# Opening of a fused decoder step: slots and banks of the first two tiles, place of the narrow tile, size of the first pieces, and who moves the raw tiles out

## The reference

```
n = x * rsqrt(mean(x * x) + 1e-6) * g_mix          # D = 2048
proj = n @ w_in     # 5,216 columns: q, k, v, qi, ki, wi (indexer), qb, kb, vb, gb, rb (GLA), uc, vc (gMLP)
```

## Time and profile before

| | |
|---|---|
| median of three runs | 1409.0 us (1406.78 to 1410.85) |
| the profiled execution, time | 1407.28 us |
| the profiled execution, span from first to last instruction | 1405.6 us |
| TensorE busy | 1393.0 us |
| VectorE busy | 850.4 us |
| ScalarE busy | 578.7 us |
| granted TensorE clock, mean | 1.00 |

### The profile page before, as it was taken

How to read it: one execution, slowest core, us unless ns; L and a number is a source line. 1 busy time by engine, 2 the same in 40 slices (tenths; PEclk the granted TensorE clock), 3 DMA queues, 4 the chain that set the end, 5 groups by cost and what they waited for, 6 DMA issues and landing times.

```text
span 1405.6 us, 28379 instructions
## 1 busy us (share of the span) xinstructions
PE 1393.0 (99%) x10632; PEld 1375.3 (98%) x10632; DVE 850.4 (61%) x1175; ACT 578.7 (41%) x696; POOL 118.8 (8%) x178
## 2 busy tenths in 40 slices
PE   7999999999999999999999999999999999999998
PEld 7999989999999999999999999999999999999998
DVE  6668767646876555555554444555555556666554
ACT  6545743565334333333333333333333333335332
POOL 1314105000221000000000000000000001111000
PEclk9999999999999999999999999999999999999999
DMA  8847434446544544544445556444544445556553
GB/s 281 226 154 241 164 123 136 147 130 233 178 155 156 179 165 157 173 158 168 156 147 164 165 163 199 158 168 157 171 157 168 159 131 164 164 164 201 176 161 117
DMA packets 76134, 236.69 MB, mean 168 GB/s; under 512 B 13800, under 2 KB 14456, under 8 KB 75704
## 3 DMA queue, kind: packets, MB, share of 16 engines
q1 hardware_dynamic: 71424, 223.59, 48.3%
q0 software_dynamic: 3776, 11.54, 2.7%
q10 hardware_dynamic: 888, 0.93, 0.2%
HBM read 231.48 MB, written 4.47 MB: 168 GB/s over the span
## 4 chain that ended last, share of the span: by engine, by line
PE 98%; DMA 1%; DVE 1%; SPq 0%; ACT 0%; issue 0%; DVEq 0%
PE acc L495 31%; PE acc L497 31%; PE acc L496 31%; PE px L1611 1%; DMA proj<-in_xT 1%; PE px L1496 0%; PE px L1574 0%; PE px L1555 0%; DMA w_raw<-in_w_in 0%; PE px L495 0%; PE px L497 0%; PE px L496 0%; DVE x_lo L1003 0%; PE px L1680 0%; PE px L1567 0%; PE px L1531 0%
## 5 line engine op out<-in xcount | busy, mean ns | idle before, releaser
L445 DVE TENSOR_TENSOR w_lo<-w_raw,w_hi 128x1024 fp32r<-128x1024 f32 (+3 forms) x446 | 507.7, 1143 | 315.6 <-ACT w_hi L439 307.0
L439 ACT ACTIVATE w_hi<-w_raw 128x1024 fp32r<-128x1024 f32 (+3 forms) x446 | 439.5, 989 | 562.7 <-PE acc L497 551.3
L495 PE MATMUL acc<-n_hi,w_hi 128*128 128x288 f32 x1664 | 492.8, 296 | 0.0
L496 PE MATMUL acc<-n_lo,w_hi 128*128 128x288 f32 x1664 | 490.9, 295 | 0.0
L497 PE MATMUL acc<-n_hi,w_lo 128*128 128x288 f32 x1664 | 489.3, 294 | 0.0
L497 PEld LDWEIGHTS acc<-n_hi,w_lo 128*128 128x128 f32 x1664 | 313.5, 188 | 0.0
L496 PEld LDWEIGHTS acc<-n_lo,w_hi 128*128 128x128 f32 x1664 | 312.4, 188 | 0.1
L495 PEld LDWEIGHTS acc<-n_hi,w_hi 128*128 128x128 f32 x1664 | 311.8, 187 | 0.1
L495 PE MATMUL acc<-x_hi,w_hi 128*128 128x288 f32 x816 | 246.5, 302 | 1.0 <-DVE w_lo L445 1.0
L496 PE MATMUL acc<-x_lo,w_hi 128*128 128x288 f32 x816 | 240.8, 295 | 0.0
L497 PE MATMUL acc<-x_hi,w_lo 128*128 128x288 f32 x816 | 240.1, 294 | 0.0
(11 more groups left out here) (283 smaller groups left out, 861.0 us busy)
## 6 DMA issues: line engine op xcount, KB each, us to landing
w_raw<-in_w_gu SPq DMA_DIRECT2D x176, 512.0 KB, 3.8
w_raw<-in_w_in SPq DMA_DIRECT2D x76, 512.0 KB, 4.3
w_raw<-in_w_down SPq DMA_DIRECT2D x64, 384.0 KB, 3.0
w_raw<-in_w_down SPq DMA_DIRECT2D x64, 320.0 KB, 3.0
w_raw<-in_w_ple SPq DMA_DIRECT2D x32, 576.0 KB, 3.8
w_raw<-in_w_out SPq DMA_DIRECT2D x32, 512.0 KB, 4.2
w_raw<-in_w_in SPq DMA_DIRECT2D x12, 256.0 KB, 6.7
proj<-in_xT SPq DMA_DIRECT2D x4, 576.0 KB, 7.5
```

Of the source, the lines that this page charges most:

```text
L439: nc.scalar.activation(whi[:, slot, 0:kt * P], raw[:, slot, 0:kt * P], ACT.Copy).then_inc(S("w_hi_done"), 1)
L445: nc.vector.tensor_tensor(wlo[:, slot, 0:kt * P], raw[:, slot, 0:kt * P], whi[:, slot, 0:kt * P].bitcast(F32), ALU.subtract).then_inc(S("w ...
L495: nc.tensor.matmul(out, w_h, row_of(m_hi_, k0 + k), start=first and k == 0, stop=False)
L496: nc.tensor.matmul(out, w_h, row_of(m_lo_, k0 + k), start=False, stop=False)
```

## The change

- The gains are loaded by ScalarE's queue under a semaphore of their own, so `small_loaded` counts to 16.
- `BEGIN` cuts the first x piece in two: rows 0 and 1 with a quarter of tile 0, rows 2 and 3 with one of tile 1. TensorE waits for each row by itself, and begins with blocks 0 and 1 of tile 0.
- The quarters of the first two tiles use the slots in the order of use: slot 0 has the first two quarters of tile 0, slot 1 those of tile 1, slots 2 and 3 the second two. The counts of `w_lo_done` and `w_used` follow.
- Tiles 0 and 1 accumulate in banks of `px`; tile 2 in `acc` bank 1, tile 3 in bank 0.
- The narrow tile is the fourth (tile 3) instead of the third; `ki` lands in turn 3.
- ScalarE moves tiles 0, 1 and 2 out unscaled, between squares and roundings, and calls Ln once on a dummy before the root.
- VectorE scales the three raw rows in one instruction, which counts `acc_read` up by 3. The remainder of chunk 8 now precedes the last squares.
- `mean_squares(0)` moves from behind chunk 6 to the middle of chunk 8.
- `weights` and SyncE's copy wait for `acc_read` of the `ki` tile, which is 4.

```diff
@@ -46,10 +46,10 @@
-ORDER = (ROW_QI, ROW_QI + 1, ROW_KI, *range(ROW_QI + 2, ROW_QI + 8), *range(ROW_K, ROW_K + 4), *range(ROW_Q, ROW_Q + 8),
+ORDER = (ROW_QI, ROW_QI + 1, ROW_QI + 2, ROW_KI, *range(ROW_QI + 3, ROW_QI + 8), *range(ROW_K, ROW_K + 4), *range(ROW_Q, ROW_Q + 8),
...
-SOURCE = (0, 1, MISC_TILE, *range(2, 8), *range(18, 22), *range(10, 18), *range(22, N_ROWS))
+SOURCE = (0, 1, 2, MISC_TILE, *range(3, 8), *range(18, 22), *range(10, 18), *range(22, N_ROWS))
...
@@ -312,7 +312,7 @@
-        SQ = ROW_QI + 2
+        SQ = ROW_QI + 3
...
@@ -445,21 +445,19 @@
+        BEGIN = [(0, 2, [(0, 0)]), (2, 4, [(1, 0)])] + [(4 * c, 4 * c + 4, [(0, c), (1, c)]) for c in range(1, 4)]
         def quarter(weights, t, c):
...
-            return weights[:, 2 * t + c // 2, (c % 2) * 4 * P:(c % 2 + 1) * 4 * P]
+            return weights[:, 2 * (c // 2) + t, (c % 2) * 4 * P:(c % 2 + 1) * 4 * P]
...
         def quarter_hi(t, c):
...
-        QUARTER_LO = {(0, 0): ("quarter_lo", 1), (1, 0): ("quarter_lo", 2), (0, 1): ("w_lo_done", 1), (1, 1): ("quarter_lo", 3),
-                      (0, 2): ("quarter_lo", 4), (1, 2): ("quarter_lo", 5), (0, 3): ("w_lo_done", 2), (1, 3): ("w_lo_done", 4)}
         def quarter_lo(t, c):
...
-            name, value = QUARTER_LO[t, c]
-            return S(name), value
+            return (S("w_lo_done"), c + t) if c % 2 else (S("quarter_lo"), c + t + 1)
...
@@ -543,13 +541,11 @@
-            sp.dma_start(gains[:, :, :], a["gains"]).then_inc(S("small_loaded"), 16)
-            for c in range(4):
-                sp.dma_start(x_f[:, 4 * c:4 * c + 4, :], a["xT"][:, 4 * c:4 * c + 4, :]).then_inc(S(f"x_loaded{c}"), 16)
-                for t in range(2):
+            for k0, k1, parts in BEGIN:
+                sp.dma_start(x_f[:, k0:k1, :], a["xT"][:, k0:k1, :]).then_inc(S(f"x_loaded{k0}"), 16)
+                for t, c in parts:
...
-                        .then_inc(loaded[2 * t + c // 2] if c % 2 else S(f"w_quarter{t}{c}"), 16)
+                        .then_inc(loaded[2 * (c // 2) + t] if c % 2 else S(f"w_quarter{t}{c}"), 16)
...
@@ -560,7 +556,7 @@
                 if c == 3 * NSLOT + 1:
-                    sp.wait_ge(S("raw_scaled"), 2)
+                    sp.wait_ge(S("acc_read"), kept(ROW_KI))
...
@@ -596,7 +592,7 @@
-            pool.wait_ge(S("x_ready"), 4)
+            pool.wait_ge(S("x_ready"), KT)
             pool.wait_ge(S("x_sq"), 2)
...
@@ -738,24 +734,33 @@
+            def keep_raw(t):
+                act.wait_ge(S("w_used"), 6 if t == 2 else 3 + t)
+                A(proj[:, ORDER[t], :], acc[:, 1, 0:T] if t == 2 else px[:, t, 0:T], ACT.Copy).then_inc(S("raw_kept"), 1)
+            act.dma_start(gains[:, :, :], a["gains"]).then_inc(S("gains_loaded"), 16)
...
-            act.wait_ge(S("small_loaded"), 16)
-            for c in range(4):
-                act.wait_ge(S(f"x_loaded{c}"), 16)
-                for k in range(4 * c, 4 * c + 4):
+            act.wait_ge(S("gains_loaded"), 16)
+            for k0, k1, parts in BEGIN:
+                act.wait_ge(S(f"x_loaded{k0}"), 16)
+                for k in range(k0, k1):
...
-                for t in range(2):
-                    act.wait_ge(loaded[2 * t + c // 2] if c % 2 else S(f"w_quarter{t}{c}"), 16)
-                    done, value = quarter_hi(t, c)
+                for t, c in parts:
+                    act.wait_ge(loaded[2 * (c // 2) + t] if c % 2 else S(f"w_quarter{t}{c}"), 16)
+                    done, _ = quarter_hi(t, c)
...
             split_hi(act, "in", 1, 0)
+            split_hi(act, "in", 1, 1)
             for c in range(2):
                 A(proj[:, SQ + 8 * c:SQ + 8 * c + 8, :], x_f[:, 8 * c:8 * c + 8, :], ACT.Square).then_inc(S("x_sq"), 1)
-                split_hi(act, "in", 1, c + 1)
-            split_hi(act, "in", 1, 3)
-            for c in range(2):
-                split_hi(act, "in", 2, c)
+                keep_raw(c)
+                split_hi(act, "in", 1, c + 2)
+            keep_raw(2)
+            split_hi(act, "in", 2, 0)
+            split_hi(act, "in", 2, 1)
+            A(epsw[:, :], ones[:, 0:1], ACT.Ln)
             root(0)
...
@@ -997,17 +1002,18 @@
-            for c in range(4):
-                for k in range(4 * c, 4 * c + 4):
+            for k0, k1, parts in BEGIN:
+                for k in range(k0, k1):
...
-                    ins = V.scalar_tensor_tensor(x_lo[:, k, :], x_f[:, k, :], gains[:, 0, k:k + 1],
-                                                 x_hi[:, k, :].bitcast(F32), ALU.mult, ALU.subtract)
-                ins.then_inc(S("x_ready"), 1)
-                for t in range(2):
+                    V.scalar_tensor_tensor(x_lo[:, k, :], x_f[:, k, :], gains[:, 0, k:k + 1],
+                                           x_hi[:, k, :].bitcast(F32), ALU.mult, ALU.subtract).then_inc(S("x_ready"), 1)
+                for t, c in parts:
...
-                        .then_inc(done, 2 if (t, c) == (1, 3) else 1)
+                        .then_inc(done, 1)
+            split_lo(dve, "in", 1, 0)
+            split_lo(dve, "in", 1, 1)
...
             def squares(first, other, n):
...
@@ -1019,35 +1025,24 @@
-            def keep_raw(t):
-                dve.wait_ge(S("w_used"), 2 * t + 2)
-                V.tensor_copy(proj[:, ORDER[t], :], acc[:, (t + 1) % 2, 0:T]).then_inc(S("acc_read"), 1)
-            split_lo(dve, "in", 1, 0)
-            keep_raw(0)
             dve.wait_ge(S("x_sq"), 1)
             link(squares(SQ, SQ + 4, 4))
-            split_lo(dve, "in", 1, 1)
-            keep_raw(1)
+            split_lo(dve, "in", 1, 2)
             dve.wait_ge(S("x_sq"), 2)
             link(squares(SQ + 8, SQ + 12, 4))
-            split_lo(dve, "in", 1, 2)
+            split_lo(dve, "in", 1, 3)
+            split_lo(dve, "in", 2, 0)
             link(squares(SQ, SQ + 8, 4))
             link(squares(SQ, SQ + 2, 2))
             V.tensor_tensor(ssq[:, :], proj[:, SQ, :], proj[:, SQ + 1, :], ALU.add).then_inc(S("x_ssq"), 1)
-            split_lo(dve, "in", 1, 3)
-            keep_raw(2)
-            split_lo(dve, "in", 2, 0)
...
-            dve.wait_ge(S("small_loaded"), 32)
+            dve.wait_ge(S("small_loaded"), 16)
...
             dve.wait_ge(S("root_ready"), 1)
-            dve.wait_ge(S("acc_read"), 3)
-            for first, n in ((ROW_QI, 2), (ROW_KI, 1)):
-                raw_rows = proj[:, first:first + n, :]
-                V.tensor_tensor(raw_rows, raw_rows, rstd[:, :].unsqueeze(1).broadcast_to([P, n, T]), ALU.mult)                    .then_inc(S("raw_scaled"), 1)
-            dve.wait_ge(S("raw_scaled"), 2)
+            dve.wait_ge(S("raw_kept"), 3)
+            raw_rows = proj[:, ROW_QI:ROW_QI + 3, :]
+            V.tensor_tensor(raw_rows, raw_rows, rstd[:, :].unsqueeze(1).broadcast_to([P, 3, T]), ALU.mult)\
+                .then_inc(S("acc_read"), 3)
             for half in range(NSLOT + 2, FIRST_STAGE):
...
@@ -1424,13 +1419,19 @@
-            def group(name, i, j, out, hi_, lo_, ready=lambda k: None, after=lambda q: None):
+            def group(name, i, j, out, hi_, lo_, ready=lambda k: None, after=lambda q: None, between=None):
                 n_parts = len(stream[name][2])
                 for q in range(n_parts):
...
                     pe.wait_ge(S("w_lo_done"), G + 1)
-                    products(out, slot, k0, kt, hi_, lo_, first=q == 0, last=q == n_parts - 1).then_inc(S("w_used"), 1)
+                    at = 0
+                    if between and q == 0:
+                        at = kt // 2
+                        products(out, slot, k0, at, hi_, lo_, last=False)
+                        between()
+                    products(out, slot, k0 + at, kt - at, hi_, lo_, first=q == 0 and not at, last=q == n_parts - 1, at=at)\
+                        .then_inc(S("w_used"), 1)
                     after(q)
...
@@ -1442,37 +1443,31 @@
-            for c in range(4):
-                ks = range(4 * c, 4 * c + 4)
-                pe.wait_ge(S("x_hi_ready"), 4 * c + 4)
-                for t in range(2):
-                    out, w_h, w_l = acc[:, 1 - t, 0:T], quarter(whi, t, c), quarter(wlo, t, c)
-                    pe.wait_ge(*quarter_hi(t, c))
-                    for k in ks:
-                        M(out, w_h[:, k % 4 * P:k % 4 * P + P], x_hi[:, k, :], start=k == 0, stop=False)
-                    pe.wait_ge(S("x_ready"), c + 1)
-                    for k in ks:
-                        M(out, w_h[:, k % 4 * P:k % 4 * P + P], x_lo[:, k, :], start=False, stop=False)
-                    pe.wait_ge(*quarter_lo(t, c))
-                    for k in ks:
-                        ins = M(out, w_l[:, k % 4 * P:k % 4 * P + P], x_hi[:, k, :], start=False, stop=k == KT - 1)
-                    if (t, c) in ((0, 1), (0, 3)):
-                        ins.then_inc(S("w_used"), 1)
-            ins.then_inc(S("w_used"), 2)
-            tile_free("in", 1, 2, 0)
```

(37 more changed lines are left out.)

## The result

| | before | changed |
|---|---|---|
| median of seven runs | 1407.21 us | 1414.00 us |
| profiled execution, span | 1405.6 us | 1412.4 us |

The ratio is 1.0045, with a 95% interval of 1.0036 to 1.0055: slower by 6.8 us, clear of noise. I had given "no change" 8 in 10 and 1411.2 us, with 1414.0 as the end of the range. That the measured median lies on this end is luck: the range was counted up from 1409.0 us, and seven runs of the kernel before have a median of 1407.21. As a difference, +6.8 us is beyond the +5.0 of the range and beyond the 4.2 us that I had called "no change". Rival A, the clock, is what happened, on top of a sum that was 1.5 us too small.

The account below looks back on a forecast made before the run. TensorE, busy 1393.0 of 1405.6 us, was taken as the bound. Gains of 2.7 us at start and stalls against 4.9 us of new waits gave +2.2 us: 1411.2 us from a median of 1409.0, range 1407.5 to 1414.0.

Parts of the forecast that it names:

- Rival A: The 4.1 us wait at `weights` drops TensorE to half clock for 3 us, costing 1.4 us: 1412.6 us; chance 0.18.
- Waits of the old kernel: TensorE's stall before chunk 5 at 26.87 us and chunk 6's lateness vanish: -1.15 and -0.25 us.
- The start: First two tiles end at 21.2 us against 22.51, x pieces coming 0.46 us earlier: -1.3 us, bounds -0.85 and -1.7.
- Chunk 8 at 31.4 us: Chunk 8's transfer, behind the narrow chunks, lands at 31.4 us, bounds 30.4 and 32.4; its rounding follows.
- rival B: Narrow chunks hold the queue longer and chunk 8 lands after 33.4 us; at 34, +4.8 us, 1413.8 us; chance 0.10.
- The chain of 6.26 us: From the start of `mean_squares` through root, Exp and chunk 10's remainder to the end of `keep(3)`: 6.26 us.
- +2.2 at `weights`: `weights` starts at 42.7 us against 40.43, waiting for `keep(3)`: +2.2 us, bounds +1.0 and +3.3.
- Copy of KI: SyncE's copy, issued at 42.7 us, lands at 46.6, wanted at 47.5: hidden by 0.9 us, cost taken as 0.
- narrow chunks: Chunks 6 and 7, ready at 26.5 and 30.0 us, needed at 27.6 and 30.8: hidden, with 0.8 us left.
- evictions on ScalarE: Three evictions moved from VectorE to ScalarE, 0.45 us each: nothing of them lies on the path.

Follow-up runs that it names:

- the filler: Changed kernel with 26 extra products, results unused, on TensorE ahead of the wait of `weights`: 1411.22 us, ratio 1.0028 against the kernel before.
- `keep(3)` first: Changed kernel with `keep(3)` right behind the scaling of the raw rows on VectorE, ahead of chunk 10's remainder: 1411.09 us, ratio 1.0024 against the kernel before.

## Where the prediction was right, and where it was wrong

The number ended inside the range by luck, as said with the result. Of the mechanism, the chain, the wait and the old stalls were right; two terms were mis-sized, and the clock, a rival that the sum left out, made almost half of the loss.

- **Waits of the old kernel.** -1.15 and -0.25 us for the slots: right; the slots alone took 1.5 us off the span.
- **The start, -1.3 us: mis-sized, -0.24 measured.** I shifted the x pieces by 0.46 us as if only issue time and bytes counted. They came at 9.34 and 13.39 us instead of 8.82 and 12.36; TensorE idled 0.66 us at 15.78. The experiments put a delay of the second piece of 0.4 to 1 us on the pieces of two. Why smaller transfers delay a later one is not settled.
- **Chunk 8 at 31.4 us: mis-sized, rounded at 32.90.** It was outside my bounds (30.4 to 32.4 for its landing). I had filled the hole in the transfers with chunk 5 and forgotten how long the queue of SyncE is held behind narrow chunks: constants went out at 24.6 us, against 23.03 before, and at 20.12 in the changed kernel with the narrow tile third. The start has a share: with the narrow tile fourth but x in four pieces chunk 8 was rounded at 30.96 and 31.94, with the tile third but pieces of two at 30.70; the two together make it late. It is rival B in a smaller size. The Trainium skill (DMA: Bandwidth & Descriptors, Why small descriptors are slow) says that transfers in rows of 256 bytes run under the full rate; the trace agrees, 155 to 188 GB/s while the narrow chunk went and 445 soon after the earlier trace rows. It moved `ssq` and so the sum of squares from 36.4 to 37.8.
- **The chain of 6.26 us: right**, 6.23 measured, Exp's table load of 1.28 us included. The rule of the Trainium skill of one load for both (ScalarE: Activation LUTs, Table sets: the hidden batching unit) again did not hold: a load stands at 39.14, right behind Ln. The dummy Ln took one load off the chain, as reckoned. The wait was 3.9 us for 4.1 forecast.
- **+2.2 at `weights`**: became +3.7, all of it the 1.4 us by which the sum of squares was late. The missing 1.1 us of the start came out of idle time: TensorE stood at the sum of squares at 37.2 instead of 35.6 us, and still waited 0.6 there. Of these 1.6 us, 0.3 is a pause for chunk 8 at 35.37.
- **The clock: the step that failed.** The sum put it at nothing. I gave its fall 0.18, argued from the end of the trace, and priced it 1.4 us, from 3 us at half clock; here half clock lasted from 44.8 to 51.6 us. It fell in every profiled execution with 2.1 us or more of idleness at `weights`, and cost 3.1 us here (7.95 less 4.82). It is needed to pass 0.3%: the filler took 2.8 us off. The Trainium skill (TensorE: Matmul & The Clock Gate, HAM oscillation) says that a long enough idle gap puts the engine back to half clock for the next work; the trace agrees, with a granted clock of 0.50 after the 3.9 us, though the first products after the gap still ran at full speed.
- **Copy of KI, narrow chunks, evictions on ScalarE**: hidden, as forecast.

Added up: 3.7 + 3.1 = 6.8 us, the measured difference.

## What to carry to other kernels

Where a stage is moved, count the work that stands between it and its input on every engine; a chain of 6 us needs 6 us of matmuls, and an engine that arrives earlier only waits longer. Price an idle gap of TensorE of 2 us and more at itself plus up to 3 us of half clock after it, and do not count on a shorter one being free: with waits of 0.6 to 0.8 us half of the executions lost clock in one kernel (`weights` one chunk later), and none with waits of 0.5 to 0.9 in another (the filler). Put transfers in short rows where nothing stands behind them in the queue, and check whether a smaller first transfer really brings the next one sooner.

## What the runs showed of the hardware

- The price of the clock is not in proportion to the gap: idle 2.1 us cost 3.2 us in the profiled execution (to `index` 8.0), 2.4 cost 1.6, 3.5 cost 1.6, 3.9 cost 3.1; and the same kernel paid 0, 1.2 or 3 us from one execution to the next.
- The kernel before, with its one stall of 1.0 us, lost clock too in some executions: a mean of 0.998 or 0.999 in 5 of 31 and 5 of 25 on two chips, in none of 33 on a third. On the first two chips all 20 executions counted for the two kernels without that stall (slots by use, with and without the gains) had 1.000. That the stall made the difference is not shown.
- The clock fell not in the gap but after work had come back: in the changed kernel it is still 1.00 to 44.0 us and 0.91 in the microsecond after, with work back at 44.12; with the narrow tile third it was down before 42 us, with work back at 41.01, and with `keep(3)` first only near 44.6 us, with work back at 42.18.
- With half the bytes per transfer ScalarE could start on x 1.2 us sooner (4.01 against 5.18 us with the gains on its own queue, 4.31 against 5.49 with them on SyncE's), and the next full piece came 0.4 and 0.7 us later in these pairs, 1 us in the means.
